# Block form with seven products for the output layers of both SwiGLU blocks

## What is computed

```python
def _swiglu(h, w_in, w_out):
    gate, up = jnp.split(h @ w_in, 2, axis=-1)
    return (jax.nn.silu(gate) * up) @ w_out
...
        x = x + _swiglu(_rmsnorm(x, norm2[i]), w_ffn_in[i], w_ffn_out[i])
```

## Time and profile before

| | |
|---|---|
| median of 3 runs | 2202.23 us (2198.14 to 2206.52) |
| profiled execution, span | 2199.4 us |
| PE busy in it | 2087.7 us (95%) |
| DVE, ACT, POOL busy | 1133.5, 830.0, 278.4 us |
| output product of layer 0, end of the input product to the next product | 594.45 to 709.50 us |
| the same of layer 1, with the memory's keys and values | 1364.10 to 1506.50 us |

### The profile page before, as it was taken

The page is one execution under the profiler, slowest core; times in us unless marked ns, Lnnn a source line. Parts: engine busy times, 40 slices in busy tenths (PEclk is TensorE's granted clock), DMA queues, the critical chain, the costliest instruction groups (busy, mean ns, idle before and its releaser), DMA issues.

```text
span 2199.4 us, 36353 instructions
## 1 busy us (share of the span) xinstructions
PE 2087.7 (95%) x15617; PEld 1133.7 (52%) x15617; DVE 1133.5 (52%) x1744; ACT 830.0 (38%) x1350; POOL 278.4 (13%) x343
## 2 busy tenths in 40 slices
PE   7998899999999999899999999999998989999998
PEld 3666554444444344689844444454565435444444
DVE  4875755454433466665544545334746465655221
ACT  4334764222222665332242223233435335323122
POOL 2321331000001010222210000001012122000000
PEclk9999999999999999999999999999999999999999
DMA  6451003333222312000023332331420021332220
GB/s 153 122 154 39 2 1 101 110 96 104 96 98 89 96 56 77 21 23 4 3 83 109 96 106 98 113 125 58 134 77 20 20 77 57 98 115 96 97 95 38
DMA packets 203843, 173.61 MB, mean 79 GB/s; under 512 B 20416, under 2 KB 179332, under 8 KB 203684
## 3 DMA queue, kind: packets, MB, share of 16 engines
q1 hardware_dynamic: 202778, 170.34, 25.4%
q10 hardware_dynamic: 906, 0.96, 0.2%
HBM read 169.18 MB, written 2.10 MB: 78 GB/s over the span
## 4 chain that ended last, share of the span: by engine, by line
PE 81%; DVE 8%; ACT 6%; issue 4%; POOL 1%; DMA 0%; ACTq 0%; DVEq 0%; SPq 0%; POOLq 0%
PE banks L1145 44%; PE banks L1192 17%; PE banks L1467 5%; PE banks L1246 2%; ACT w_hi L1753 1%; PE banks L1479 1%; PE banks L1266 1%; DVE w_lo L2320 1%; PE banks L1224 1%; PE banks L1655 1%; PE banks L1207 1%; ACT arena L1855 1%; PE banks L1579 1%; PE banks L1305 1%; ACT arena L2154 1%
## 5 line engine op out<-in xcount | busy, mean ns | idle before, releaser
L1145 PE MATMUL banks<-arena,w_hi 128*128 128x512 f16 (+1 forms) x2160 | 628.2, 374 | 8.0 <-DVE arena L2340 3.8
L2320 DVE TENSOR_TENSOR w_lo<-wring,w_hi 128x2048 bf16<-128x2048 f32 (+3 forms) x162 | 357.5, 2208 | 463.5 <-ACT w_hi L1753 461.6
L1753 ACT ACTIVATE w_hi<-wring 128x2048 f16<-128x2048 f32 (+3 forms) x162 | 294.7, 1822 | 436.3 <-PE banks L1192 255.3
L1145 PE MATMUL banks<-arena,w_lo 128*128 128x512 f16 (+1 forms) x1080 | 403.9, 374 | 0.0
L1192 PE MATMUL banks<-arena,w_hi 128*128 128x512 f16 x1216 | 361.6, 379 | 2.2 <-DVE arena L2613 1.1
L1145 PEld LDWEIGHTS banks<-arena,w_hi 128*128 128x128 f16 x2160 | 211.2, 98 | 254.7 <-issue 7.0
L993 POOL TENSOR_TENSOR arena<-arena,ntmp 128x512 f32<-128x512 f32 (+1 forms) x79 | 101.9, 1290 | 1246.9 <-ACT ntmp L1783 1240.6
L1192 PE MATMUL banks<-arena,w_lo 128*128 128x512 f16 x608 | 230.4, 379 | 0.0
L1145 PE MATMUL banks<-h_hi,w_hi 128*128 128x512 f16 (+1 forms) x576 | 219.5, 381 | 6.9 <-DVE w_lo L2320 5.5
L1145 PE MATMUL banks<-h_lo,w_hi 128*128 128x512 bf16 (+1 forms) x576 | 219.2, 381 | 0.0
L1145 PE MATMUL banks<-h_hi,w_lo 128*128 128x512 f16 (+1 forms) x576 | 219.1, 380 | 0.0
(11 more groups left out here) (404 smaller groups left out, 2732.8 us busy)
## 6 DMA issues: line engine op xcount, KB each, us to landing
wring<-in_w_ffn_in SPq DMA_DIRECT2D x88, 512.0 KB, 4.9
wring<-in_w_ff SPq DMA_DIRECT2D x32, 1024.0 KB, 5.1
wring<-in_w_ffn_out SPq DMA_DIRECT2D x20, 1024.0 KB, 4.9
wring<-in_rw_w_in SPq DMA_DIRECT2D x11, 1024.0 KB, 5.1
wring<-in_w_in SPq DMA_DIRECT2D x11, 1024.0 KB, 5.0
wring<-in_nsa_w_in SPq DMA_DIRECT2D x7, 1024.0 KB, 6.6
wring<-in_w_mem_kv SPq DMA_DIRECT2D x4, 1024.0 KB, 5.2
wring<-in_w_o SPq DMA_DIRECT2D x4, 1024.0 KB, 5.0
```

The lines of the kernel that those rows point to most:

```text
L1145: last = mm(v, p[0], p[1], start=(i == 0), stop=(i == len(prods) - 1))
L1753: A(w_hi[:, at[0] % NSPLIT, 0:w["size"]], wring[:, w["slot"], 0:w["size"]], ACT.Copy).then_inc(split_hi, 1)
L2320: V.tensor_tensor(w_lo[:, sl, 0:w["size"]], wring[:, w["slot"], 0:w["size"]], w_hi[:, sl, 0:w["size"]], ALU.subtract).then_inc(split_lo, 1)
```

## The change

The output product is computed as a 2 x 2 block product with seven block products in place of eight (the form of Strassen and Winograd). The two sides of the split are: the 2816 hidden features, of which block i and block i + 11 make a pair (`FP` = 11, and the input product runs in the order `PAIRED`); the 512 tokens, in two halves of 256; and the 1024 output features, of which two neighbouring blocks of 128 make a pair (`out_pair`, four pairs `pr`).

- **Hidden side.** A pair of hidden blocks gives four 128 x 256 quarters. DVE writes them into `QB` and forms four sums of them (`pair_mixed`: one operation of 512 and two of 256 columns), ACT and DVE split the seven operands in one operation of 1792 columns each (`pair_high`, `pair_low`), per two jobs.
- **Weight side.** A panel holds four 128-column blocks of up to four weight rows of blocks (kk = 4, 4, 3 for each pair of outputs, so 12 panels a layer, as many as before), moved by four transfers. Of it, 3/4 are split as they are (step 0, "plain"). Then POOL forms four sums in the ring slot itself (`weights_summed`: one addition of 2 x 128 x kk columns, then two of 128 x kk, each waiting for the one before). The first waits until DVE has split step 0; ACT splits the first two sums (step 1) when the first addition is done and the other two (step 2) when all three are. Each panel takes two entries of the `w_hi`/`w_lo` ring, one for step 0, one for steps 1 and 2.
- **PE** (`paired_sum`): 7 x kk x 3 matmuls of 256 columns per panel, 7 x 11 x 3 x 4 = 924 a layer, in the order: three plain products (after step 0), two of step 1, two of step 2.
- **Output side.** ACT copies one bank to SBUF (`first_copied`), DVE combines the four banks (`pair_added`: five operations of 256 and one of 512 columns) and adds to two blocks of `xT` (two operations of 512 columns), for each output pair.
- **Program order.** ACT and DVE issue all three steps of panel n + 1 while PE reads panel n (`split_next`). The high parts and squares of the pair before (`normed`) stand on ACT after the splits of the second panel of a pair; `pair_added` stands on DVE after the splits of the next pair's first panel. In layer 1 the memory's products come between pair 1 and pair 2.

```diff
+FP = FT // 2
+PAIRED = [i + FP * hf for i in range(FP) for hf in range(2)]
...
+            for u, cut, opens, sums in ((plain_u, lambda v: v[:, 0:3, :], True, None),
+                                        (sum_u, lambda v: v[:, 0:4:3, :], True, "first"),
+                                        (sum_u, lambda v: v[:, 1:3, :], False, "second")):
...
+        def out_pair(w_dram, pr):
+
+            ts = [tile("v") for _ in range(2)]
+            ps = [(summed_panel(w_dram, pr, k0, min(4, FP - k0)), k0, min(4, FP - k0)) for k0 in range(0, FP, 4)]
+            b_ = [4, 6, 7, 5] if pr % 2 else [(ts[0].n + i) % NBANK for i in range(4)]
+            return dict(n=pr, ts=ts, ps=ps, banks=[b_[0], b_[3], b_[1], b_[2]])
...
+            def weights_summed(w):
+
+                st = w["steps"][1]
+                q4, ns = st["raw"], st["nsum"]
+                pool.wait_ge(split_lo, st["m"])
+                nc.gpsimd.tensor_tensor(q4[:, 0:4:3, :], q4[:, 0:2, :], q4[:, 3:4, :].broadcast_to([P, 2, q4.shape[2]]),
+                                        ALU.add).then_inc(w_sum, 1)
+                pool.wait_ge(w_sum, ns + 1)
+                nc.gpsimd.tensor_tensor(q4[:, 1, :], q4[:, 1, :], q4[:, 0, :], ALU.add).then_inc(w_sum, 1)
+                pool.wait_ge(w_sum, ns + 2)
+                nc.gpsimd.tensor_tensor(q4[:, 2, :], q4[:, 2, :], q4[:, 1, :], ALU.add).then_inc(w_sum, 1)
...
+                        pe.wait_ge(split_lo, w["steps"][0]["m"] + 1)
+                        product(w, w["plain"], 1, k0, kk, 0, x0, 0)
+                        product(w, w["plain"], 2, k0, kk, 1, x2, 0)
+                        product(w, w["plain"], 0, k0, kk, 6, x3, 0).then_inc(panel_read, 1)
+                        pe.wait_ge(split_lo, w["steps"][1]["m"] + 1)
+                        last = product(w, w["summed"], 0, k0, kk, 3, x0, 1)
+                        if ends:
+                            last.then_inc(first_done, 1)
+                        product(w, w["summed"], 3, k0, kk, 4, x1, 1)
+                        pe.wait_ge(split_lo, w["steps"][2]["m"] + 1)
+                        last = product(w, w["summed"], 1, k0, kk, 5, x1, 0)
+                        if ends:
+                            last.then_inc(acc_full, 1)
+                        product(w, w["summed"], 2, k0, kk, 2, x2, 1).then_inc(acc_full if ends else panel_read, 1)
...
-                    act.wait_ge(landed[w["slot"]], w["level"])
-                    if at[0] >= NSPLIT:
-                        act.wait_ge(*splits[at[0] - NSPLIT]["read"])
-                    A(w_hi[:, at[0] % NSPLIT, 0:w["size"]], wring[:, w["slot"], 0:w["size"]], ACT.Copy).then_inc(split_hi, 1)
+                    raw, hi, _ = w["flat"]
+                    if w["sums"] is None:
+                        act.wait_ge(landed[w["slot"]], w["level"])
+                    else:
+                        act.wait_ge(w_sum, w["nsum"] + (1 if w["sums"] == "first" else 3))
+                    if w["opens"] and w["unit"]["n"] >= NSPLIT:
+                        act.wait_ge(*units[w["unit"]["n"] - NSPLIT]["read"])
+                    A(hi, raw, ACT.Copy).then_inc(split_hi, 1)
...
+                    for i in range(len(pr["ps"])):
+                        split_to(split_next(pairs, pr, i))
+                        if i == 0 and pr["n"] and not (pr["n"] == 2 and f is ffn[1]):
+                            normed(pairs[pr["n"] - 1])
...
+            def pair_added(l, pr):
...
+                dve.wait_ge(acc_full, ts[0].n + 1)
+                link(V.tensor_tensor(u2, x1[:, 0, :], p1, ALU.add))
+                V.tensor_tensor(y_, u2, p5, ALU.add)
+                link(V.tensor_tensor(u3, x1[:, 1, :], u2, ALU.add))
+                V.tensor_tensor(c22, u3, p5, ALU.add)
+                dve.wait_ge(acc_full, ts[1].n + 1)
+                V.tensor_tensor(c21, x3[:, 0, :], u3, ALU.add)
+                link(V.tensor_tensor(pair_t[:, 0:4:2, :], x2, pair_t[:, 0:4:2, :], ALU.add))
+                for x_, c_, sc in ((sets(xT[:, k, :]), pair_t[:, 0:4:2, :], 1.0 / PROD_SCALE),
+                                   (sets(xT[:, k + 1, :]), pair_t[:, 5:7, :], -1.0 / PROD_SCALE)):
+                    V.scalar_tensor_tensor(x_, c_, sc, x_, ALU.mult, ALU.add).then_inc(evac_v, 1)
```

More of the change, by code:

```diff
@@ L311, in block_stack, with unit @@
         panels = []
-        splits = []
+        splits, units = [], []
+        def unit():
+            u = dict(n=len(units), read=None, at=len(units) % NSPLIT)
+            units.append(u)
+            return u
         def panel(*srcs):
@@ L1072, in _ @@
             pool.nop().then_inc(consts, 1)
[L1073 to L1075 removed]
+            paired(ffn[1])
             read_out(pool, xd_tiles)
@@ L1173, in gemm, with paired_sum, product @@
                         then[n]()
+            def paired_sum(f):
+                nm, jobs, pairs, l, then = f
+                for pr in pairs:
+                    ts, ps, (x0, x1, x2, x3) = pr["ts"], pr["ps"], pr["banks"]
+                    if pr["n"] == 2 and f is ffn[1]:
+                        gemm(mem2_jobs[0:1], mem2_norm)
+                        read_out(pe, pairs[1]["ts"][0:1])
+                        row_sums(mem2_norm)
+                        gemm(mem2_jobs[1:], mem2_norm)
+                    if pr["n"] == 2 and f is ffn[0] or pr["n"] == 3:
+                        read_out(pe, pairs[pr["n"] - 2]["ts"][0:1])
+                    if pr["n"] == 3 and f is ffn[1]:
+                        pe.wait_ge(d_root, mem2_norm["r"] + 1)
+                    begun_banks = set()
+                    def product(w, u, i, k0, kk, st, b, hf):
+                        if b not in begun_banks and (pr["n"] == 0 or pr["n"] == 2 and f is ffn[1]):
+                            read_out(pe, [tiles[ts[0].n - NBANK + (b - ts[0].n) % NBANK]])
+                        v = bank[b][:, hf * M:hf * M + M]
+                        for k in range(kk):
+                            wk = w["w"](u, i, k)
+                            for a_, b_ in ((0, 0), (0, 1), (1, 0)):
+                                last = mm(v, wk[a_], pair_in[b_][k0 + k][:, st, :], start=b not in begun_banks,
+                                          stop=(w is ps[-1][0] and k == kk - 1 and a_ == 1), skip_group_check=True)
+                                begun_banks.add(b)
+                        return last
+                    for w, k0, kk in ps:
+                        ends = w is ps[-1][0]
+                        if pr["n"] == 0:
+                            pe.wait_ge(q_lo, l * FP + k0 + kk)
+                        pe.wait_ge(split_lo, w["steps"][0]["m"] + 1)
[12 more added lines that the diff above has]
+                        product(w, w["summed"], 2, k0, kk, 2, x2, 1).then_inc(acc_full if ends else panel_read, 1)
@@ L1994, in swiglu_act @@
                                 by_token(t, dst, v, tts, 8)
-                    ready(k)
-                    high(then, k)
-                    if k < 4 or f is ffn[0]:
-                        square(then, k)
+                        split_to(pr["ps"][0][0]["steps"][2]["m"])
+                    for i in range(len(pr["ps"])):
+                        split_to(split_next(pairs, pr, i))
+                        if i == 0 and pr["n"] and not (pr["n"] == 2 and f is ffn[1]):
+                            normed(pairs[pr["n"] - 1])
+                    if f is ffn[1] and pr["n"] == 0:
+                        act.wait_ge(d_lo, mem2_norm["c"] + KC)
+                    if pr["n"]:
+                        act.wait_ge(evac_v, pairs[pr["n"] - 1]["ts"][1].order + 1)
+                    act.wait_ge(first_done, 4 * l + pr["n"] + 1)
+                    A(pair_t[:, 0:2, :], sets(bank[pr["banks"][0]][:]), ACT.Copy).then_inc(first_copied, 1)
+                normed(pairs[3])
                 if f is ffn[1]:
```

258 lines of the change are left out of this document (182 added, 76 removed).

## The result

| | before | after |
|---|---|---|
| median | 2203.59 us (4 runs, 2198.14 to 2206.52) | 2247.43 us (4 runs, 2243.32 to 2249.19) |
| span of the profiled execution | 2199.4 us | 2246.6 us |
| layer 0, end of the input product to the row sums of the next norm | 120.2 us | 142.2 us |
| layer 1, the same, with the memory's keys and values | 158.4 us | 177.9 us |

The change makes the kernel slower by the ratio 1.0202 (95% interval 1.0183 to 1.0221). The two output stages, each taken up to the sums over partitions behind it, account for 22.0 + 19.5 = 41.5 us.

What follows compares the result with a forecast made beforehand. TensorE bounds the kernel before; after, the round of a weight panel does. Layers +22.5 and +19.9 and clock +3.4 make +45.8 us on 2199.4, 2245.2; the median stands 2.8 above, so 2248 us, range 2216 to 2272.

Steps and rivals of the forecast that it cites:

- the round of a weight panel: Output product: splits and additions following one another per panel, 10.25 us (kk = 4) or 8.1 (kk = 3); TensorE needs 9.18, 6.89.
- the first rival: Output product: the weights' splits and additions are hidden and TensorE stays the bound; 2187 us, 0.7% faster; chance 9%.
- TensorE's work, 12.9 us less a layer: Output product: 924 matmuls of 256 columns take 101.0 us against 113.9 for 528 of 512.
- GpSimd's additions, 2.41, 1.27, 1.27 us: Weight sums of a kk = 4 panel: the first addition about 2.41 us, each other 1.27, bounds 10% either way.
- The hold of 0.50 us: VectorE's low part of step 1 and GpSimd's third addition hold each other up: 0.50 us a panel, bounds 0 and 1.1.
- `pair_added`, 4.2 us net: End of an output pair: VectorE's eight operations delay step 0 of the panel after by 4.2 us, waits included.
- The stages: Output stages: last matmul at 133.4 us in layer 0; layer 1's pairs end at 156.7; with end waits, 137.5 and 162.3.
- The waits at the end, 4.1 and 5.6 us: Behind each layer's output product: TensorE waits for the last blocks of `xT`, 4.1 us in layer 0, 5.6 in layer 1.
- The clock, 3.4 us: TensorE's clock falls to half after long waits; taken as 2 x 1.7 = 3.4 us in all.
- The signs to look for: Output product: TensorE about 75% busy, waits ahead of L1253, 3.6 us a pair, ScalarE waiting for GpSimd twice a panel.
- The clock did not stay down: Rival: in both output stages the clock falls and stays at half; some +185 us, 2387 us; chance 3%.
- the third rival: Output product: the chain rules but is much shorter, GpSimd at 80%, small operations cheaper too; +12 us, 2214; chance 4%.

Runs made afterwards that it cites:

- run 1: The changed kernel without GpSimd's three additions (it only signals, so the output is not the right one): 2186.94 us.
- run 3: The changed kernel with one more wait, so that VectorE makes the low part of step 1 only after GpSimd's three additions: 2229.73 us.

## Why the prediction was right

The sign, the size (2248 against 2247.43) and the place came out: the round of a weight panel rules, GpSimd's additions are what makes it long, and `pair_added` and the high parts lengthen it. Without the additions the time is 2186.9, which is the 2187 that the first rival gave for "TensorE stays the bound"; the decision lay where that rival put it, in the price of the additions. But the fit within 1 us is closer than the terms were, and some of it is luck:

- **TensorE's work, 12.9 us less a layer**: 0.110 us a matmul where nothing holds it up (run 1). Right.
- **GpSimd's additions, 2.41, 1.27, 1.27 us**: 2.34, 1.27, 1.26 without a meeting (run 3). Right.
- **The hold of 0.50 us**: mis-sized. 0.86 was measured (2.13 less 1.27). I took the one meeting in the trace before as a price; the hold follows what is left of VectorE's operation when the addition starts: 0.50 with 0.64 us left in the earlier trace rows, 0.59 with 0.74 left in the smaller panels (1.59 less 1.00), 0.86 with 1.00 left in the large ones. The rule of the Trainium skill that the prediction weighed gave 0.9, and it was the better estimate.
- **`pair_added`, 4.2 us net**: 3.85 in the timeline. The operations of 256 columns take 0.42 each and overlap by some hundredths. The hand-overs were some tenths of a us cheaper too. These errors and that of the hold offset each other: I had 35.3 us a pair; the long waits of TensorE fall at 637.82, 672.32 and 707.82, so 34.5 and 35.5.
- **Meetings with the sums of squares**: a term that the prediction lacked, and the 1.0 us between those two pairs. From the second pair of outputs on, VectorE's low parts for the next norm, and the low part of step 0 behind them, meet GpSimd's sums of squares (GpSimd's rows first):

```profile
680.54 1.84 POOL L1074 TENSOR_TENSOR arena<-arena,ntmp 128x512 f32<-128x512 f32 x1 [2.30 <-ACT ntmp L1936]
682.52 1.53 POOL L1074 TENSOR_TENSOR arena<-arena,ntmp 128x512 f32<-128x512 f32 x1
```

```profile
681.16 1.76 DVE L2515 SCALAR_TENSOR_TENSOR h_lo<-xT,cols,h_hi 128x512 bf16<-128x512 f32 x1
682.85 2.41 DVE L2496 TENSOR_TENSOR w_lo<-wring,w_hi 128x1152 bf16<-128x1152 f32 x1
```

  The first time, when GpSimd has one such sum to make and not two, the same low part takes 0.75 us (at 646.66), and from this panel's first addition to the next panel's it is 12.0 us and not 13.0.
- **The stages**: 133.4 forecast and 133.2 measured in layer 0, 156.7 and 156.5 in layer 1, the idle 5.9 us at its start included. In layer 1 two errors offset each other: its panels 4 and 5 started 2.9 and 2.7 us earlier than forecast (48.2 and 62.1, not 51.1 and 64.8), and panel 6, behind the memory's products, at 99.7, not 99.4.
- **The waits at the end, 4.1 and 5.6 us**: oversized. They are 1.04 + 1.04 + 0.86 + 0.30 = 3.24 us in layer 0 and 1.04 + 2.90 = 3.94 in layer 1. The main ones:

```profile
735.61 0.39 PE L1253 MATMUL banks<-h_hi,w_hi 128*128 128x512 f16 x1 [1.04 <-DVE h_lo L2515]
...
1552.78 0.39 PE L1253 MATMUL banks<-h_hi,w_hi 128*128 128x512 f16 x1 [2.90 <-DVE h_lo L2515]
```

- **The clock, 3.4 us**: half right. Behind the 2.90 us the granted clock was half for 3.4 us, worth 1.7 us. The falls at layer 1's start and behind two of the three waits of 2.73 us in layer 0 left no mark on the stages: TensorE had that much less to wait behind them. But the clock was half also from 1465.4 to 1472.2, in the memory's products, where TensorE does not wait. From the row sums of the memory's norm on, that stretch took 22.5 us (1465.43 to 1487.93), and 19.2 in run 1, where the clock was whole: some 3.3 us that the prediction put at nothing. By stretch (length, PE, PEld, DVE, ACT, POOL, clock):

```profile
1554.20:1557.60 3.40, 3.40 (x10) 1.20 (x9) 0.00 (x0) 1.59 (x3) 2.97 (x4) 0.51 0.00 0
...
637.90:641.30 3.40, 3.40 (x32) 3.05 (x33) 0.00 (x0) 1.06 (x1) 3.32 (x2) 1.00 0.00 0
673.60:677.00 3.40, 3.40 (x18) 2.47 (x17) 1.19 (x1) 1.06 (x1) 3.24 (x3) 0.52 0.00 0
```

- **The sum.** By the terms, +45.8 us. The stages gave +41.5; the other 5.7 of the profiled execution's 47.2 lie in stretches that the change does not touch: 1.8 ahead of layer 0, 0.4 between the layers, 3.5 behind. The same stretches vary in the other runs: 648.4 to 655.0 us between, 677.3 to 681.1 behind. So 4 us of the agreement are chance. The medians are 43.8 us apart, and the one before came out 1.4 above the 2202.23 that the forecast started from.
- **The signs to look for.** TensorE's busy share fell to 82% and 86% in the two stages, not to 75%; the waits for low parts stand before L1306, the line of the output product, and not before L1253; the long wait of a pair was 2.73 us, not 3.6. ScalarE's two waits for GpSimd a panel, and none for TensorE, came as told. The gain possible at most is 25.9 + 1.1 = 27 us by the prediction's own terms, not 28.
- **The other rivals.** The clock did not stay down: 0.97 and 0.95 of the full clock were granted over the two stages. The additions and `pair_added` were not cheap enough for the third rival either: 4.9 us for the three additions of a large panel without a meeting, against 4.95 forecast.

## What to carry to other kernels

Before moving arithmetic from a full engine to the idle ones, write down the round: what must follow what for one unit of work, each with its duration on its engine, and compare that with the time the full engine needs for the unit. Engines at 55% can be the bound when they mostly work in turn, and the repair is then to shorten the ring (here by giving a step to the busier but faster engine that already holds the data), not to balance load. And a move that fills an idle time is worth something only while that idle time exists; once the engine runs ahead again, an instruction that waits for TensorE must not stand in front of the work that keeps it ahead.
